# Mixer products read two slots later, and 72 expert rows added on VectorE in five ranges of slots

## The reference

```python
    ue = u_tab[eidx]                    # gathered rows, 1024 wide
    ve = v_tab[eidx]
    h = gelu(einsum('td,thkd->thk', xb, ue))
    return einsum('thk,thkd->td', gate * h, ve)
```

## Time and the profile before

| | before |
|---|---|
| median of 3 runs | 4105.85 us (4105.6 to 4116.54) |
| the profiled execution | 4106.0 us |
| span of its trace | 4104.3 us, mean granted clock 0.945 |
| TensorE / VectorE / ScalarE / GpSimd busy | 81% / 63% / 34% / 33% |
| gathers | 1152, 1208 MB |
| first gather use to the end | 880 us to 4104 us |

### The profile page before, as it was taken

One profiled execution on the slowest core, in us unless ns is written; L12 is line 12 of the kernel. 1 busy time (PEld: TensorE's weight loads), 2 busy tenths in 40 slices (PEclk: granted clock), 3 DMA queues, 4 the chain that ended last, 5 costly groups with the idle time before them and its releaser, 6 DMA issues.

```text
span 4104.3 us, 35864 instructions
## 1 busy us (share of the span) xinstructions
PE 3305.3 (81%) x10378; PEld 1714.6 (42%) x10378; DVE 2582.6 (63%) x6376; ACT 1375.2 (34%) x4074; POOL 1366.8 (33%) x1218
## 2 busy tenths in 40 slices
PE   8875599787777777799977987898788987777777
PEld 4443499452232232156533642553334532232222
DVE  0088555117667666666887557579776667667665
ACT  1144222013333333332456333324553322333332
POOL 0021000014444444444432334344334433444433
PEclk9987699799999999999999999999899999999999
DMA  3100000239999999999988999999899999999998
GB/s 124 35 1 6 1 1 2 67 142 387 421 421 418 420 418 406 416 372 358 381 326 300 382 335 421 387 385 416 307 349 419 416 407 422 421 421 416 419 420 355
DMA packets 229846, 1284.89 MB, mean 313 GB/s; under 512 B 23569, under 2 KB 73745, under 8 KB 82065
## 3 DMA queue, kind: packets, MB, share of 16 engines
q0 software_dynamic: 165888, 1208.03, 72.8%
q1 hardware_dynamic: 63760, 74.57, 5.4%
HBM read 1278.12 MB, written 3.87 MB: 312 GB/s over the span
## 4 chain that ended last, share of the span: by engine, by line
DMA 32%; PE 32%; issue 5%; DVE 5%; ACT 5%; POOL 1%; DVEq 0%; POOLq 0%; ACTq 0%; SPq 0%
DMA ring<-in_uv,route 27%; PE banks L1505 22%; PE banks L1826 3%; DMA own<-in_l_w_in 3%; DVE ring L1445 2%; PE banks L2312 2%; PE banks L1877 2%; ACT route L1490 1%; PE banks L1884 1%; DMA own<-in_l_peer_wq 1%; ACT L1475 1%; ACT route L1475 1%; DMA own<-in_l_w_out 1%; ACT L1955 1%; ACT route L1480 1%
## 5 line engine op out<-in xcount | busy, mean ns | idle before, releaser
L1505 PE MATMUL banks<-ring,route 128*128 128x512 f32 (+1 forms) x4512 | 2178.0, 619 | 540.3 <-ACT route L1490 529.8
L1445 DVE SCALAR_TENSOR_TENSOR ring<-ring,XN 128x1024 f32<-128x1024 f32 x1152 | 1409.4, 1223 | 812.3 <-DMA ring<-in_uv,route 801.2
L1434 POOL DMA_INDIRECT ring<-in_uv,route x1152 | 1267.9, 1101 | 1908.3 <-PE banks L1505 1708.3
L1505 PEld LDWEIGHTS banks<-ring,route 128*128 128x128 f32 (+1 forms) x4512 | 809.4, 189 | 1650.4 <-issue 839.5
L1475 ACT ACTIVATE route<-route 128x2 f32<-128x2 f32 x576 | 116.6, 202 | 1467.3 <-DVE ring L1445 1463.7
L1490 ACT ACTIVATE route<-IDN,route 128x128 f32<-128x128 f32 x1000 | 339.8, 386 | 3.1 <-PE banks L1505 2.8
L1480 ACT ACTIVATE route<-route 128x1 f32<-128x1 f32 x1152 | 276.7, 287 | 23.2
L1826 PE MATMUL banks<-own,QP 128*128 128x225 f32 (+2 forms) x800 | 186.8, 369 | 27.8 <-DMA own<-in_l_w_in 27.8
L1826 PEld LDWEIGHTS banks<-own,QP 128*128 128x128 f32 x800 | 153.8, 193 | 95.6 <-issue 89.0
L111 POOL TENSOR_TENSOR ys<-ys,IDN 128x4 f32<-128x4 f32 x9 | 9.1, 1008 | 385.7 <-DVE ys L1188 385.7
L1475 ACT ACT_TABLE_LOAD x105 | 134.7, 1283 | 1.9
(11 more groups left out here) (411 smaller groups left out, 3362.8 us busy)
## 6 DMA issues: line engine op xcount, KB each, us to landing
ring<-in_uv,route POOLq DMA_INDIRECT x1152
own<-in_l_peer_wq SPq DMA_DIRECT2D x9, 1024.0 KB, 12.2
own<-in_l_w_in SPq DMA_DIRECT2D x8, 1024.0 KB
own<-in_l_w_out SPq DMA_DIRECT2D x8, 1024.0 KB
own<-in_l_w_in SPq DMA_DIRECT2D x8, 900.0 KB
W<-in_l_w_in SPq DMA_DIRECT2D x2, 2560.0 KB, 21.6
X<-in_x_prompt SPq DMA_DIRECT2D x8, 512.0 KB, 8.3
WO<-in_l_w_out SPq DMA_DIRECT2D x4, 1024.0 KB, 9.0
```

What stands on the lines that cost most here:

```text
L1434: pool.indirect_dma_start(self.ring[:, s % RING, :], None, self.io[f"uv{of_slot(s)[0]}"], bass.IndirectOffsetOnAxis(ap=self.EI[:, g % 2, k ...
L1445: dve.scalar_tensor_tensor(u, u, 1.0, self.XN[:, of_slot(s)[1], :], ALU.mult, ALU.mult, accum_out=self.HD[:, g % 2, k:k + 1]).then_inc(sel ...
L1505: m = pe.matmul(self.bank[1 + half][0:n, :], self.DG[:, (V_TENSOR[s] - 1) % 4, 0:n], self.ring[:, s % RING, D + 512 * half:D + 512 * half ...
```

## The change

1. `SHARES` is no longer empty. In slots 334 to 403 each third down row goes to VectorE (23), in 492 to 536 each second (22), in 590 to 649 each fourth (15), in 770 to 801 each fourth (8), in 816 to 847 each fourth, of which only 4 count, since from slot 832 on the pass is that of tile 4. That makes 72 rows more on VectorE, 96 in all.
2. VectorE adds its rows sooner: the rows of slots e and e+1 (e even) both at index e+2, after that slot's dot, where it was e+3 and e+4.
3. In `plan` the readers of TensorE's results come later against the products: "project" from 0.6 to 2 slots, and the products themselves start at 10 and not at 8; relu, "soft", "finish", "out_turn", "add", query copies each by about 1 to 1.8. PSUM banks rotate for turns, heads and index scores, where each had one.
4. Plan numbers follow: preparation 2.5 to 3 slots later, attention of tile 0 two later (96), output 168.5 from 167, queries 201.2 from 200 with 1.4 slots each from 1.55.

```diff
--- before.py
+++ after.py
@@ -1284,7 +1284,7 @@
     return any(a <= s < b and s % every == every - 1 for a, b, every in SHARES)
 
 
-SHARES = []
+SHARES = [(334, 404, 3), (492, 537, 2), (590, 650, 4), (770, 802, 4), (816, 848, 4)]
 V_VECTOR = [sum(on_vector(i) for i in range(s + 1)) for s in range(S_ALL)]
 V_TENSOR = [s + 1 - V_VECTOR[s] for s in range(S_ALL)]
 
@@ -1643,13 +1643,13 @@
                 dve.append((x + 4, "scale", w, i))
                 for b in range(2):
                     pe.append((x + 5 + b, "turn", w, i, b))
-                    act.append((x + 5.8 + b, "xt", w, i, b))
+                    act.append((x + 6.6 + b, "xt", w, i, b))
         for s in range(NC + ND):
             for i in range(nt):
                 n = s * nt + i
                 for k in range(KD):
-                    pe.append((8 + (n + k / KD) * c, "in", n, k))
-                act.append((8 + (n + 1) * c + .6, "project", n))
+                    pe.append((10 + (n + k / KD) * c, "in", n, k))
+                act.append((10 + (n + 1) * c + 2, "project", n))
         for i in range(nt):
             a, b = prep + 3 * i, prep + 3 * nt + 8 * i
             for k in range(3):
@@ -1663,54 +1663,54 @@
             pool.append((x + 3, "v_root", i))
             for k in range(2):
                 dve.append((x + 5 + .7 * k, "settle", i))
-            pe.append((x + 7, "mix", i))
+            pe.append((x + 6.5, "mix", i))
             for k in range(2):
                 dve.append((x + 8 + .5 * k, "gate", i, k))
         for i in range(nt):
             x = heads + gap * i
             for b in range(5):
                 pe.append((x + b, "heads", i, b))
-                act.append((x + b + .6, "heads", i, b))
+                act.append((x + b + 1.6, "heads", i, b))
             for h in range(8):
                 pe.append((x + 6 + h, "index", i, h))
-                act.append((x + 6.6 + h, "relu", i, h))
-                dve.append((x + 7.2 + h, "score", i, h))
+                act.append((x + 7.6 + h, "relu", i, h))
+                dve.append((x + 8.2 + h, "score", i, h))
             for r in range(SEL_KEYS[self.tiles[i]] // 8):
-                dve.append((x + 15 + top[i] * r, "top", i, r))
+                dve.append((x + 16 + top[i] * r, "top", i, r))
             if SEL_KEYS[self.tiles[i]]:
-                dve.append((x + 15 + top[i] * SEL_KEYS[self.tiles[i]] / 8, "mask", i))
+                dve.append((x + 16 + top[i] * SEL_KEYS[self.tiles[i]] / 8, "mask", i))
             for h in range(8):
                 y = att[i] + pace * h
                 pe.append((y, "scores", i, h))
-                dve.append((y + .7, "soft", i, h))
-                act.append((y + 1.4, "exp", i, h))
-                pe.append((y + 2.2, "probs", i, h))
-                act.append((y + 3, "probs", i, h))
-                pe.append((y + 3.7, "values", i, h))
-                dve.append((y + 4.5, "finish", i, h))
+                dve.append((y + 1.6, "soft", i, h))
+                act.append((y + 2.3, "exp", i, h))
+                pe.append((y + 2.7, "probs", i, h))
+                act.append((y + 4.3, "probs", i, h))
+                pe.append((y + 4.7, "values", i, h))
+                dve.append((y + 6.3, "finish", i, h))
             for b in range(2):
                 pe.append((out - 6 + 2 * i + b, "out_turn", i, b))
-                act.append((out - 5.4 + 2 * i + b, "out_turn", i, b))
+                act.append((out - 4.4 + 2 * i + b, "out_turn", i, b))
             for j in range(NO):
                 n = j * nt + i
                 for k in range(KD):
                     pe.append((out + (n + k / KD) * o, "out", n, k))
-                dve.append((out + (n + 1) * o + .6, "add", n))
+                dve.append((out + (n + 1) * o + 1.8, "add", n))
         if self.sample is not None:
-            dve.append((out + NO * nt * o + 1, "zero"))
+            dve.append((out + NO * nt * o + 2, "zero"))
             dve.append((heads + gap * self.sample, "keep_v"))
         for h in range(PH):
             for k in range(KD):
                 pe.append((query + (h + k / KD) * q, "query", h, k))
-            act.append((query + (h + 1) * q + .5, "query", h))
+            act.append((query + (h + 1) * q + 2, "query", h))
         self.todo = {}
         for name, turns in (("pe", pe), ("act", act), ("dve", dve), ("pool", pool)):
             turns.sort(key=lambda x: x[0])
             self.todo[name] = [(base + scale * x[0], *x[1:]) for x in turns]
         self.end = self.todo["act"][-1][0]
-        pick = {"turn": lambda w, i, b: 3 + b, "in": lambda n, k: 5 + n % 3, "mix": lambda i: 7, "heads": lambda i, b: 3,
-                "index": lambda i, h: 4, "scores": lambda i, h: 5, "probs": lambda i, h: 6, "values": lambda i, h: 7,
-                "out_turn": lambda i, b: 3 + b, "out": lambda n, k: 5 + n % 3, "query": lambda h, k: 5 + h % 3}
+        pick = {"turn": lambda w, i, b: 3 + (2 * i + b) % 4, "in": lambda n, k: 5 + n % 3, "mix": lambda i: 7, "heads": lambda i, b: 3 + (5 * i + b) % 2,
+                "index": lambda i, h: 3 + h % 2, "scores": lambda i, h: 5, "probs": lambda i, h: 6, "values": lambda i, h: 7,
+                "out_turn": lambda i, b: 3 + (2 * i + b) % 3, "out": lambda n, k: 5 + n % 3, "query": lambda h, k: 5 + h % 3}
         self.at = {}
         for x in self.todo["pe"]:
             kind, key = x[1], x[2:]
@@ -2395,8 +2395,9 @@
                     if PASSES.index((1, 4)) in (j for j in range(len(PASSES)) if ENDS[j - 1] == s):
                         dve.wait_ge(one.xd.h, one.xd.at(16))
                     ex.dve_dot(dve, s)
-                if s >= 3 and on_vector(s - 3):
-                    ex.dve_weigh(dve, s - 3)
+                for late in (2, 1):
+                    if late <= s < S_ALL + late and (s - late) % 2 == late % 2 and on_vector(s - late):
+                        ex.dve_weigh(dve, s - late)
                 if s in ENDS:
                     pending = ENDS.index(s)
                 if s - 2 in ENDS:
@@ -2412,10 +2413,10 @@
     st.close()
 
 
-PLAN_A = dict(scale=1.0, c=2.3, prep=50, heads=80, gap=16, top=[0, .95, 1.1], att=[94, 126, 142], pace=2.0, norm2=189,
-              out=167, o=1.9, query=200, q=1.55, ln=78)
-PLAN_B = dict(scale=1.0, c=3.0, prep=46, heads=72, gap=34, top=[1.3, 1.8], att=[114, 152], pace=3.0, norm2=224,
-              out=190, o=4.0, query=236, q=4.0, ln=69)
+PLAN_A = dict(scale=1.0, c=2.3, prep=53, heads=80, gap=16, top=[0, .95, 1.1], att=[96, 126, 142], pace=2.0,
+              norm2=189.5, out=168.5, o=1.9, query=201.2, q=1.4, ln=81.5)
+PLAN_B = dict(scale=1.0, c=3.0, prep=48.5, heads=72, gap=34, top=[1.3, 1.8], att=[114, 152], pace=3.0, norm2=224,
+              out=190, o=4.0, query=236, q=4.0, ln=72.5)
 
 
 # ---- launch: one core; inputs and outputs as the reference has them ----
```

## The result

The changed kernel takes 4041.08 us (median of 4 runs, 4038.24 to 4045.94), the kernel before 4105.73 (4 runs, 4101.12 to 4116.54): ratio 0.984, 95% interval 0.9818 to 0.9862, faster by 65 us.

A forecast was written before the change was run, and what follows sets the result against it. Gathers' DMA pace bounds slots without a mixer; TensorE, slab loads and engines waiting in turn hold the mixer windows. Terms 12 + 7 + 3 + 8 + 7 + 4 + 3 + 13 = 57 us off 4106.0 give 4049 us, range 3992 to 4094.

The forecast's parts named there:

- Later readers: Mixer windows, slots 416 to 480 and 656 to 768: moving waits later gains 3, 8, 7, 3 and 13 us, 34 in all.
- TensorE 47.9 busy of 59.3, at most 11.4: Slots 464 to 480, attention: TensorE's idle time caps the later readers' gain at 11.4 us; 8 was taken.
- The DMA share: Mixer windows: free time read from DMA share against 1.01, 12.9 us in 464 to 480, 21.5 in 704 to 768.
- The bytes' 19.0 and 36.3: Slots 464 to 480 and 704 to 768: excess over the floor for gathers and slab bytes, 19.0 and 36.3 us.
- the prediction's floors: Mixer windows: 2.52 us per slot plus 2.97 us per MB of slab, 232.7 us for slots 336 to 416.
- VectorE's cap: Slots 448 to 464: VectorE busy 54.8 of 59.0 us, so at most 4.2 us to gain; 3 was taken.
- Moved rows: Down rows moved to VectorE gain 12 us from slot 334, 7 in 492 to 536, 4 in 590 to 649, 0 from 770.
- the rival: Slabs and DMA take the down rows' gain, only later readers give; gain 12 to 35 us, about 4083; chance 0.18.
- The sign that the rival had named: Slots 352 to 400: if the slab rival holds, over half of the chain is `in_l_w_in`.
- the forecast's sign of being wrong downward: At L1455: VectorE shows idle time before it, ended by ScalarE.
- that rival: Slower: VectorE stands at the new rows, deciding at 0.8 us uncovered per row; at 1.5 us, 4157 us; chance 0.08.
- The clock rival: Gaps left by moved rows drop TensorE to 1.2 GHz some 30 times, losing 51 us, about 4098; chance 0.03.

The follow-up runs named there:

- run 336: Not a label: "slabs in one run", then slots 336 to 416. Changed kernel with each partition's slab laid out as one run: 3986.39 us, ratio 0.9706.

## Why the prediction was right, and where it was not

The forecast of 4049 us was 8 above the measured 4041; by the profiled executions, 57 us were forecast and 60 came. The sum is better than its terms.

**Later readers: the mechanism was right, two terms were mis-sized.** Forecast 3, 8, 7, 3 and 13, measured 2.2, 18.6, 5.7, 6.5 and 24.2, in all 57 for 34. That it is the attention readers is shown: putting back six offsets takes all 49 us of the change without moved rows, and three of the five stretches (58.4, 134.9 and 200.2 us) are then as before. The step that failed is "TensorE 47.9 busy of 59.3, at most 11.4". Busy time was not work. For the same 16 slots TensorE is busy 40.0 us in the changed kernel. Its down rows there, before and after (count: shortest, median and longest record in ns; then busy us and mean ns):

```profile
L1505 PE MATMUL banks<-ring,route x64: 592/593/1222, 2183.8 to 2239.6; 128*128 128x512 f32 x64
...
L1505 PE MATMUL banks<-ring,route 128*128 128x512 f32 x64 | 35.3, 679 | 11.2 <-ACT route L1490 11.2
```
```profile
L1505 PE MATMUL banks<-ring,route x61: 592/592/697, 2171.2 to 2211.9; 128*128 128x512 f32 x61
...
L1505 PE MATMUL banks<-ring,route 128*128 128x512 f32 x61 | 29.5, 604 | 0.0
```

The median record is the same. What made the mean longer is records of up to 1222 ns, twice the median and so at the lower clock (0.91 was granted in that window, 1.00 after), and the page counts them as busy: some 61 x 75 ns = 4.6 us on this line. The second trace of before says the same, with the clock at 0.97, a mean of 629 ns and 44.8 us busy of 56.7. The rest of the difference is mostly seven records more in the window before (145, after 138), since it is cut by VectorE's dots and TensorE runs behind them. The cap of 11.4 us, then, took slow time and work of other slots for work of these. In 704 to 768 the 13 passed no cap; it was too small a share of what was free: TensorE's idle time fell from 41.4 to 23.8 us and its busy time from 156.2 to 149.6, with the clock from 0.92 to 0.96.

The Trainium skill says in "Perfetto Trace Analysis", section "Identifying the Most-Contended Engine", that TensorE's busy share is no good measure of how near the engine is to its limit, because pipelined instructions look smaller in a trace. The trace agrees that the share misleads, though here the other way: it overstated the work.

The DMA share was no bound either: 12.9 us in 464 to 480, 21.5 in 704 to 768 and 4.0 in 656 to 704 were passed. The bytes' 19.0 and 36.3 were not, but their 4.0 in 656 to 704 was, by 2.5 us. With slabs in one run 336 to 416 and 592 to 656 end below the prediction's floors too (230.4 against 232.7, 183.4 against 189.4), so 2.97 us per MB of slab was priced too high. VectorE's cap (4.2 us, 2.2 gained) held, as its busy time stayed 55.

**Moved rows: the rival was half right.** Forecast 12, 7, 4 and 0; measured, together with the later readers, gains of 8.1 and 7.2 and losses of 6.6 and 3.3. The experiments part them: 14 us with the slabs as they are, 0 without the later readers, 25 with slabs in one run. The forecast had named the slab ("the faster the slots run the more the slab holds them") and not given it enough: after the change it is 54% of the chain, with waits

```profile
PE banks L1826 <- DMA own<-in_l_w_in: 31.7, 4, 9.0
...
DVE X L1455 <- ACT route L1480: 21.0, 4, 7.7
```

In that window TensorE stood 31.7 us for slabs against 10.4 before, and much of the 23 x 1.72 us that it was relieved of went into them. It is so in every kernel: the page's wait for projection slabs is 61 to 72 us in the five traces with all rows moved (65.5 in the moved rows alone, where the time didn't change), 63.5 with mixer one's, 20 to 33 in the four with none, and 0 with slabs in one run. The sign that the rival had named, over half of the chain in slots 352 to 400, came out at the mark: 49% there (1818.8 to 1979.2 us), 54% in 1785 to 1930. The rival's price of 25.6 us a slab held (25.6 to 26.6), though its 4083 did not, for attention gave what it gave.

**Slots 592 to 656, wrong sign.** A gain of 4 was forecast and a loss of 6.6 came; over two traces of each kernel it is (206.0 + 201.5 - 199.4 - 192.6) / 2 = 7.8 us. With slabs in one run the stretch is 183.4 to 183.9 in all three kernels tried, so what is lost there is lost at slabs. TensorE waited for slabs there 17.4 and 13.8 us in the two traces of before, 39.7 and 35.6 in those of the changed kernel and 27.2 with the later readers alone. Why more is lost with the change stays open: neither taking back its moved rows (217.3) nor its later start (202.6) undid it, the moved rows alone had 204.6, the later readers alone 209.6, and these with attention as before 199.8. Scatter of some 7 us lies in each number.

**VectorE standing at its rows** was the forecast's sign of being wrong downward, and it came: 21.0 us, all of it in four waits of slots 336 to 416, the longest 7.7. Over 96 rows that is 0.2 each against the 0.8 from which that rival decides, and taking most of it away moved nothing. The earlier adding is worth nothing, as forecast. The clock rival was seen in small: rows of 3.37 and 3.41 us behind two of three slab waits, clock down by 0.05 to 0.06 in both slab stretches; its own sum, 4049 + 51, gives 4100 and not 4098. And where the forecast says that all but one of the mixers' windows are slower than 2.52 us a slot, all nine are.

## What to carry to other kernels

Where engines run hand-ordered streams, place each reader so many slots behind its writer that the writer's engine, with its usual lag, is done: that moved 49 us here with no instruction added or removed, and it shows in the waits as several engines standing 15 to 18 us for each other while none is full. Before moving work off an engine, look at what is next on its chain in the same stretch; here it was a prefetch with two buffers, and its cure was the layout of the source, not less work. Bound a gain by an engine's work at its full clock and by the bytes at their best measured rate, not by busy time: 40.0 us and not 47.9 here.

## What the runs showed of the hardware

A slab of 0.9 MB as 1024 runs of 900 bytes took 26 us to land beside the gathers (page of the changed kernel, KB and median us to landing):

```profile
own<-in_l_w_in SPq DMA_DIRECT2D x8, 900.0 KB, 26.1
```

As 128 runs of 7200 bytes it landed in about 8 us and was not once waited for at the projections, where 71.4 us had been lost. It was not short of bandwidth: DMA moved more per us then (411 GB/s in slots 336 to 416, against 373). Nor was it the small packets' own cost: the queue's packets took 5.5% of the 16 engines' span in the changed kernel and 5.1% with the new layout, an estimated 222 and 203 us, 19 us of engine time spread over the whole run for 55 us gained.

The Trainium skill says in "DMA: Bandwidth & Descriptors", section "Queues, rings and completion order", that each DMA engine takes turns between the queues it has work for and changes queue at packet boundaries. The trace agrees: while a slab is under way 905 of its queue's packets moved beside 905 of the gathers', and with the new layout 144 beside 161. So a slab in 1024 small packets waited for about as many large ones, 13.8% of the engines' time being its own, and one in 128 packets got 44.3%. In the kernel before, at 1840 to 1844 us, GpSimd was waiting for TensorE and the gathers had 60.3% of the engines' time; there 627 packets of a slab moved beside 140 of theirs. It is the forecast's point that a load lands soon when TensorE has fallen behind.

The lower clock showed as single records of up to 1222 ns where the median is 593, and it lengthens TensorE's busy time with no work added.
